# Seven moves in a one-core diffusion-trunk kernel: first attention scores, last head pair, first output products, last expert unit and its overflow test

## What is computed

```python
h = rmsnorm(x, g1) * (1 + sc1) + sh1          # sh, sc, gate rows from silu(cond) @ w_ada
z = h @ w_in                                   # columns of four mixers
y_f = fftn(u_f, axes=(1, 3), norm='ortho').real             # Fourier
y_l, y_s = rg_lru(...), gated_convolution(...)
q, k, v = latent_attention_inputs(...)         # 8 heads of 96; 640 keys for a latent token
o = softmax(q @ k.T * scale) @ v
br = stack([y_f @ w_pf, y_l @ w_pl, y_s @ w_ps, o @ w_pm])
out = sum(sigmoid(h @ w_gate) * br) @ w_out
x = x + gate1 * out
h = rmsnorm(x, g2) * (1 + sc2) + sh2
# top-1 of 4 groups, top-2 of its 8 experts; 32 experts of width 256
x = x + gate2 * sum_e combine_e * ((silu(h @ w1_e) * (h @ w3_e)) @ w2_e)
```

## Time and profile before

| | us |
|---|---|
| median of 3 runs | 1126.73 (1122.79 to 1127.68) |
| the profiled execution | 1123.43 |
| its span | 1121.5 |
| PE busy | 1007.0 (90%) |
| DVE busy | 388.4 (35%) |
| ACT, POOL busy | 225.3, 166.2 |
| mean granted TensorE clock | 0.959 |
| moved by DMA | 196.12 MB |

### The profile page before, as it was taken

How to read it: one execution, slowest core, us unless ns; L and a number is a source line. 1 busy time by engine, 2 the same in 40 slices (tenths; PEclk the granted TensorE clock), 3 DMA queues, 4 the chain that set the end, 5 groups by cost and what they waited for, 6 DMA issues and landing times.

```text
span 1121.5 us, 10795 instructions
## 1 busy us (share of the span) xinstructions
PE 1007.0 (90%) x4164; PEld 567.2 (51%) x4164; DVE 388.4 (35%) x845; ACT 225.3 (20%) x444; POOL 166.2 (15%) x160
## 2 busy tenths in 40 slices
PE   3899998999799989999999999989957897978875
PEld 1555544655455557777777777745533332322221
DVE  3314331135653523323233233317672232221222
ACT  3213630114254421101011011002111220211111
POOL 0000000010430013122132132100010111111111
PEclk9999999999889999999999999999978998998988
DMA  9634344100000152212213113092169999999993
GB/s 375 284 132 181 150 150 185 69 5 2 1 1 1 57 214 100 98 48 79 72 47 104 47 47 103 13 363 94 59 243 388 359 383 400 403 423 402 404 411 98
DMA packets 36163, 196.12 MB, mean 175 GB/s; under 512 B 7504, under 2 KB 11280, under 8 KB 25872
## 3 DMA queue, kind: packets, MB, share of 16 engines
q1 hardware_dynamic: 31200, 184.40, 41.9%
q0 software_dynamic: 4768, 10.50, 3.9%
q10 hardware_dynamic: 144, 0.52, 0.1%
HBM read 188.13 MB, written 14.09 MB: 180 GB/s over the span
## 4 chain that ended last, share of the span: by engine, by line
PE 82%; DMA 9%; issue 4%; DVE 3%; ACT 1%; POOL 0%; SPq 0%; POOLq 0%; DVEq 0%; ACTq 0%
PE psum L962 22%; PE psum L1143 9%; PE psum L697 8%; PE psum L979 8%; PE psum L1015 6%; PE psum L1159 4%; DMA r_bv<-in_w_e 4%; PE psum L813 3%; PE psum L899 3%; PE psum L698 2%; PE psum L706 2%; PE psum L913 2%; DMA r_w<-h_scratch,tab 2%; DMA r_w<-in_w_ada 2%; PE psum L923 2%
## 5 line engine op out<-in xcount | busy, mean ns | idle before, releaser
L962 PE MATMUL psum<-r_h,r_w 128*128 128x320 f32 x512 | 143.3, 433 | 1.7 <-DVE r_d L1824 1.7
L2248 POOL TENSOR_TENSOR r_w<-r_w 128x512 f32<-128x512 f32 x64 | 80.6, 1270 | 313.1 <-PE psum L962 237.2
L962 PEld LDWEIGHTS psum<-r_h,r_w 128*128 128x128 f32 x512 | 97.2, 190 | 42.3 <-DVE r_d L1824 2.0
L962 PE MATMUL psum<-r_ys,r_w 128*128 128x320 f32 x384 | 108.6, 432 | 0.0
L697 PE MATMUL psum<-r_h,r_w 128*128 128x512 f32 x192 | 98.9, 597 | 1.5 <-DVE r_h L1587 1.5
L962 PEld LDWEIGHTS psum<-r_ys,r_w 128*128 128x128 f32 x384 | 73.0, 190 | 30.4
L1414 ACT ACTIVATE r_bv<-r_bv 128x320 f32<-128x320 f32 x64 | 30.1, 470 | 273.2 <-DVE r_bv L1871 273.2
L1015 PE MATMUL psum<-r_w,r_bv 128*128 128x512 f32 x160 | 74.0, 609 | 3.4 <-DVE r_bv L1866 3.4
L698 PEld LDWEIGHTS psum<-r_h,r_w 128*128 128x128 f32 x192 | 36.5, 190 | 45.9 <-issue 45.9
L2259 POOL DMA_INDIRECT out_y<-r_bv,tab x17 | 26.8, 1576 | 211.7 <-DVE r_bv L2099 191.7
L979 PE MATMUL psum<-r_ys,r_w 128*128 128x320 f32 x192 | 55.6, 432 | 0.0
(11 more groups left out here) (378 smaller groups left out, 1624.4 us busy)
## 6 DMA issues: line engine op xcount, KB each, us to landing
r_a<-in_w_ada SPq DMA_DIRECT2D x8, 2048.0 KB, 7.9
r_w<-in_w_gate SPq DMA_DIRECT2D x32, 512.0 KB, 4.6
r_a<-in_w_e SPq DMA_DIRECT2D x6, 2048.0 KB, 32.3
r_c<-in_w_e SPq DMA_DIRECT2D x6, 2048.0 KB, 32.8
r_w<-in_w_e SPq DMA_DIRECT2D x5, 2048.0 KB, 35.9
r_ys<-in_w_e SPq DMA_DIRECT2D x4, 2048.0 KB, 35.4
r_bv<-in_w_e SPq DMA_DIRECT2D x4, 2048.0 KB, 37.5
r_h<-in_w_e SPq DMA_DIRECT2D x4, 2048.0 KB, 36.2
```

The lines of the kernel that those rows point to most:

```text
L962: ins = mm(gate_bank(u, n), w[:, k, :], x[:, k, :], start=(k == 0), stop=(k == HK - 1))
L2248: g.tensor_tensor(w_mix[n], x, y, op).then_inc(s_wm, 1)
```

## The change

1. `modulation(11)` moves from ahead of `fy0` to between `fy0` and `fy1`; `FRONT` changes accordingly.
2. PE's first two `scores` come ahead of the transposes `qt4`, each waiting only for its own slot's last drain; slot 2's drain is waited for at the first `probabilities_T`, `qt4`'s at the first unit that reads it. On DVE `take_queries(4)` comes behind the first two maxima. The three `prob` buffers get new homes, since `qt4`'s input is still in the old ones.
3. The last `inverse` comes behind the first `gate_product` of gate unit 0, and the waits for the mixers' outputs move to the first `branch`.
4. The first four k of the four first output pieces wait for 12 merges in place of 16, and each for its own bank (`s_gadd`); the wait for 16 stands behind them.
5. Unit 16's two `w13` are loaded as four halves, both lower halves first; the upper ones have a semaphore of their own, waited for ahead of the second half of `hidden`.
6. Unit 16 projects into slot 0 and no longer waits for `s_yd` 16; DVE copies its transposed hidden values ahead of scaling unit 15's result.
7. The overflow test comes one unit sooner, behind unit 14's `project`, on all engines; on PE it waits for `s_yd` 15. POOL's store of unit 15 moves behind the test, and the overflow body uses slot 1 in place of 3.

```diff
-                          "l11r", "l11i", "uf1", "ar10", "fa0", "fa1", "fa2", "fa3", "fa4", "ar11", "fy0", "fy1",
+                          "l11r", "l11i", "uf1", "ar10", "fa0", "fa1", "fa2", "fa3", "fa4", "fy0", "ar11", "fy1",
...
+Y_SLOT = [2] * LAST + [0]
...
-        prob = [r_t[:, 0:NT], r_t[:, NT:2 * NT], r_sq[:, 0:NT]]
+        prob = [r_t[:, H * QK:H * QK + NT], r_sq[:, 0:NT], r_d[:, 3 * NT:4 * NT]]
...
                 for i in AFTER[u]:
-                    load_w13(i)
+                    if i in AT[LAST]:
+                        load_piece(i, wexp[i % NBUF][0][:, 0:W13 // 2], 0, W13 // 2, w13_loaded[i % NBUF])
+                    else:
+                        load_w13(i)
+                for i in AFTER[u]:
+                    if i in AT[LAST]:
+                        load_piece(i, wexp[i % NBUF][0][:, W13 // 2:W13], W13 // 2, W13, w13_rest)
...
-            sp.wait_ge(s_Y, LAST)
+            sp.wait_ge(s_Y, LAST - 1)
             overflow(sp, n_x, load_chunk)
...
-            modulation(11)
             wait_drained(pe, *[f"fa{t}" for t in range(TT)])
...
             for j in range(2):
+                if j:
+                    modulation(11)
                 o = begin(f"fy{j}")
...
-            heads_T("qt4", KT + TT - 1)
-            for s in range(4):
-                pe.wait_ge(drained[s], LAST_IN_SLOT[s])
...
                 if i >= 2:
                     pe.wait_ge(s_prob, i - 1)
+                else:
+                    pe.wait_ge(drained[i], LAST_IN_SLOT[i])
+                if t == LT:
+                    wait_drained(pe, "qt4")
...
             for i in range(2):
                 scores(i)
+            heads_T("qt4", KT + TT - 1)
...
             values(H // 2 - 1)
-            inverse(H // 2 - 1, len(UNITS))
-            pe.wait_ge(s_oTd, 4)
-            pe.wait_ge(s_yl, 2)
-            pe.wait_ge(s_ys, 2)
...
                 gate_product(u, 0, w[:, 0, 0], low[:, :, lo_t])
+                if u == 0:
+                    inverse(H // 2 - 1, len(UNITS))
...
+            pe.wait_ge(s_mdone, GATE_UNITS - 4)
+            for i, added in enumerate((3, 5, 6, 7)):
+                pe.wait_ge(s_gadd, 7 * (GATE_UNITS - 1) + added)
+                output(i // 2, i % 2, range(0, 4))
             pe.wait_ge(s_mdone, GATE_UNITS)
-            for t in range(2):
-                for n in range(2):
-                    output(t, n, range(0, 4))
...
+                if u == LAST:
+                    pe.wait_ge(w13_rest, 16 * len(AT[LAST]))
                 hidden(H_SLOT[u % 2], halves, range(KD // 2, KD)).then_inc(s_A, 1)
...
-                if u:
+                if u and u < LAST:
                     pe.wait_ge(s_yd, u)
...
-                if u != LAST - 1:
+                if u != LAST - 2:
                     continue
-                pe.wait_ge(s_yd, LAST)
+                pe.wait_ge(s_yd, LAST - 1)
+                pe.wait_ge(s_xTd, LAST + 1)
                 pe.wait_ge(s_slot, 1)
                 n_x = pe.value_load(xinfo[0:1, XCH:XCH + 1], min_val=1, max_val=XCH)
...
-            take_queries(TT - 1)
...
             for i in range(2):
                 maxima(i)
+            take_queries(TT - 1)
...
+                if p == LAST - 1:
+                    take_gate_T(LAST)
                 for n in range(2):
                     ins = v.tensor_tensor(y_sb[:, p % 2, n * 512:(n + 1) * 512],
-                                          psum[:, 2, n * 512:(n + 1) * 512], slot_g2[n], ALU.mult)
+                                          psum[:, Y_SLOT[p], n * 512:(n + 1) * 512], slot_g2[n], ALU.mult)
...
-            put_rows(LAST - 1)
...
-                pool.wait_ge(y_stored[i], 16 * (LAST // 2))
+                pool.wait_ge(y_stored[i], 16 * (LAST // 2 - i))
...
             overflow(pool, n_x, chunk)
+            put_rows(LAST - 1)
             put_rows(LAST)
```

More of the change, by code:

```diff
@@ L598, in load_piece @@
                      else a["w_e"][e, :, lo:hi])
-                sp.dma_start(dst, w).then_inc(done[i % NBUF], 16)
+                sp.dma_start(dst, w).then_inc(done, 16)
             def load_w13(i):
@@ L906, in probabilities_T @@
                 n = TT if UNITS[i][1] < LT else 1
+                if i == 0:
+                    pe.wait_ge(drained[2], LAST_IN_SLOT[2])
                 pe.wait_ge(s_prob, i + 1)
@@ L976, in branch @@
                         pe.wait_ge(s_mrg, 4 * u)
+                    elif j == 0:
+                        pe.wait_ge(s_oTd, 4)
+                        pe.wait_ge(s_yl, 2)
+                        pe.wait_ge(s_ys, 2)
                     for n, part in enumerate((lo_t, hi_t)):
@@ L1151, in hidden_T, with project @@
                 return ins
-            def project(halves):
+            def project(halves, slot=2):
                 for n in range(2):
@@ L1197, in _ @@
                     pe.wait_ge(w2_loaded[i % NBUF], 16 * pieces_until(W2_PIECES, i))
-                if u:
+                if u and u < LAST:
                     pe.wait_ge(s_yd, u)
                 pe.wait_ge(s_hT, u + 1)
-                project([(lo, wexp[i % NBUF][1:], hT[:, u % 2, :, lo:lo + C]) for lo, i in zip((0, C), AT[u])]) \
+                project([(lo, wexp[i % NBUF][1:], hT[:, u % 2, :, lo:lo + C]) for lo, i in zip((0, C), AT[u])], Y_SLOT[u]) \
                     .then_inc(s_Y, 1)
-                if u != LAST - 1:
+                if u != LAST - 2:
                     continue
-                pe.wait_ge(s_yd, LAST)
+                pe.wait_ge(s_yd, LAST - 1)
+                pe.wait_ge(s_xTd, LAST + 1)
                 pe.wait_ge(s_slot, 1)
@@ L1214, in chunk @@
                     pe.wait_ge(x_w, x * 16)
-                    hidden(3, [(0, x_wexp, x_xgT)]).then_inc(x_A, 1)
+                    hidden(1, [(0, x_wexp, x_xgT)]).then_inc(x_A, 1)
                     pe.wait_ge(x_h, x)
-                    hidden_T(3, x_gate).then_inc(x_hf, 1)
+                    hidden_T(1, x_gate).then_inc(x_hf, 1)
                     pe.wait_ge(x_hT, x)
@@ L1511, in chunk @@
                     act.wait_ge(x_A, x)
-                    A(x_gate[0:C, :], psum[0:C, 3, 0:FE], ACT.Tanh, scale=0.5).then_inc(x_th, 1)
+                    A(x_gate[0:C, :], psum[0:C, 1, 0:FE], ACT.Tanh, scale=0.5).then_inc(x_th, 1)
                     act.wait_ge(x_yd, x)
@@ L2080, in hidden_dve, with take_gate_T @@
                 v.tensor_tensor(x, x, o[:, FE:2 * FE], ALU.mult).then_inc(s_hid, 1)
+            def take_gate_T(u):
+                dve.wait_ge(s_hf, u + 1)
+                v.tensor_copy(hT[:, u % 2, :, :], psum[:, H_SLOT[u % 2], 512:512 + 2 * P]
+                              .rearrange("p (f n) -> p f n", f=2)).then_inc(s_hT, 1)
             hidden_dve(0)
             for p in range(LAST + 1):
-                dve.wait_ge(s_hf, p + 1)
-                v.tensor_copy(hT[:, p % 2, :, :], psum[:, H_SLOT[p % 2], 512:512 + 2 * P]
-                              .rearrange("p (f n) -> p f n", f=2)).then_inc(s_hT, 1)
                 if p < LAST:
+                    take_gate_T(p)
                     hidden_dve(p + 1)
@@ L2110, in chunk @@
                     v.scalar_tensor_tensor(out=x_gate[0:C, :], in0=x_gate[0:C, :], scalar=1.0,
-                                           in1=psum[0:C, 3, 0:FE], op0=ALU.add, op1=ALU.mult).then_inc(x_g, 1)
+                                           in1=psum[0:C, 1, 0:FE], op0=ALU.add, op1=ALU.mult).then_inc(x_g, 1)
                     dve.wait_ge(x_g, x)
-                    v.tensor_tensor(x_gate[0:C, :], x_gate[0:C, :], psum[0:C, 3, FE:2 * FE], ALU.mult) \
+                    v.tensor_tensor(x_gate[0:C, :], x_gate[0:C, :], psum[0:C, 1, FE:2 * FE], ALU.mult) \
                         .then_inc(x_h, 1)
                     dve.wait_ge(x_hf, x)
-                    v.tensor_copy(x_hT_sb, psum[:, 3, 512:512 + 2 * P]
+                    v.tensor_copy(x_hT_sb, psum[:, 1, 512:512 + 2 * P]
                                   .rearrange("p (f n) -> p f n", f=2)[:, :, 0:C]).then_inc(x_hT, 1)
```

11 lines of the change are left out of this document (6 added, 5 removed).

## The result

The changed kernel takes **1108.24 us** (median of 4 runs, 1104.77 to 1111.29) beside 1126.74 for the kernel before: ratio 0.9849, 95% interval 0.9826 to 0.9871. The forecast was 1107.4. The profiled execution took 1108.71 with a span of 1106.8. One of all executions of the kernel before, beside the second group of experiments, took 3439 us; no ratio uses it.

The account below looks back on a forecast made before the run. PE and its waits bound the kernel up to the last output product, then a gapless weight stream and a tail. Gains of 4.3, 7.2, 1.7, 0.9 and 3.6 sum to 17.7, from 1125.1 to 1107.4 us; range 1100 to 1114.5.

Parts of the forecast that it names:

- The two regimes: Up to the last output product PE and its waits bound; from there a gapless weight stream, then a tail.
- the bound of 4.7: Upper bound for moving modulation 11 between the Fourier products, taking half of `ar11`'s 3.08 us; forecast 4.3.
- The third rival: Low clock at the attention's and output's starts: attention gives 4.2, output nothing; 3.9 us more, 1111.3; chance 0.15.
- 3 us to spare: In the tail, the last `w2` lands at 1101.6, with 3 us to spare.
- stalling jump: Rival: the moved overflow test's jump stalls PE ahead of `hidden(16)`, moving the tail by 6.3 us to 1113.7; chance 0.12.
- The sum: Gains of 4.3, 7.2, 1.7, 0.9 and 3.6 over the whole kernel add to 17.7 us.
- limit of 5.6 us: For the whole kernel's time, 0.5%, about what can be told from no change.
- fourth rival: The stream ends when it did, so only the tail's 3.6 us counts: 1121.5; chance 0.04.

Follow-up runs that it names:

- again: The changed kernel run once more without any edit; 1108.86 us, ratio 0.9852.
- m2r: The changed kernel with VectorE's wait for the two later broadcast rows moved behind its first residual addition; 1107.24 us.
- both: The changed kernel with the edits of `inside` and `m2r` together; 1105.64 us, ratio 0.9829.
- fill_both: `both` plus 18 small unused transposes on PE in the gaps ahead of the last values; 1102.61 us, ratio 0.9792.
- final: `fill_both` with the last inverse back ahead of the gates and more filling transposes in the front and at the attention's start; 1100.54 us, ratio 0.9781.
- inside: The changed kernel with PE's waits for s_yd and s_xTd moved from ahead of the overflow test into the overflow loop's body; 1108.81 us.
- early_load: `inside` with PE's load of the overflow flag moved sooner, behind unit 2's projection; 1108.69 us.
- scores_alone: The kernel before with only part 2 of the change; 1119.59 us, ratio 0.9959.
- fill_inverse_back: The changed kernel with filling transposes ahead of the last values and the last inverse back ahead of the gates; 1105.15 us.
- inverse_back: The changed kernel with the last inverse back ahead of the gates, the mixers' waits staying at the first branch; 1109.40 us.

## Why the prediction was right, step by step

**The two regimes** held. From the first streamed load to the last landing it was 278.6 before, 278.1 after, and 278.1 to 278.5 in `again`, `m2r`, `both`, `fill_both` and `final`. What was saved ahead of it moved it whole: 823.02 became 812.82. (`inside` and `early_load` had 281.0 and 279.4; `inside` shows one longer PE wait near the stream's start, 10.58 for a small transfer where `both` has 9.16; I did not follow it further.)

**Part 1**, forecast 4.3, gave 3.8. `ar11` took 1.93, as estimated; the profiles show 1.92 as its length at full clock, so the bound of 4.7, with half of 3.08, could not be reached. Of the missing 0.5, 0.3 is the gap behind `fa4` (1.09, where the step has 0.75), the rest the two `fy`, 7.48 and 7.41 instead of 7.3.

**Part 2**, forecast 7.2, gave 7.9 at its place, with scores at full clock as I chose. Its step left something out: the start of the attention was costed, its end was taken to follow unchanged. The last values lost 2.45 and the two short transposes ahead of them 0.3. `scores_alone` shows that loss to come with part 2: 4.6 net in time. What in part 2 brings it, the earlier start or the new buffers, stays open, and for the kernel before there is only one profile with the full clock there. The third rival (the clock falls where I keep it up) was right in kind and named the wrong places.

**Part 3**, forecast 1.7, gave 1.5 (the shift grew from 8.07 at the end of the last values to 9.52 at the end of the gates). The size was right and the cause wrong. The step gave the gain to the inverse's new place; the traces of `fill_inverse_back` and `inverse_back` have no gap ahead of the gates with the inverse back in its old place, so the waits' new place gives it, and the inverse's costs 0.3.

**Part 4**, forecast 0.9, gave 0.7: the shift grew from 9.52 at the end of the gates to 10.20 at the stream's start. The gap of 2.7, its cause and the slow products behind it (four took 3.58, the next four 1.88) came as worked out. `m2r` confirms the cause.

**Parts 5 to 7**, forecast 3.6, gave 4.1: `project(14)` ended 10.57 sooner, the end came 14.7 sooner. The order was as forecast: a gap of 2.86 (2.9 forecast), no gap ahead of `hidden_T(16)`, a projection of 3.65 instead of 5.37. Two steps were not right. The halves are worth 0.1 to 1.6 and not nothing. And the last `w2` did not have 3 us to spare in every execution: in `again` it was what ended last.

The **stalling jump** did not show. Scaling to `hidden(16)` took 1.28 with full DMA queues, 1.32 before with empty ones, and no time at all once the waits were gone. The Trainium skill's rule in "Runtime: NRT & Kernel Launch", Instruction fetch mechanics, speaks of a target outside what is fetched; no run here shows such a stall.

**The sum.** In the profiled pair: 3.8 + 7.9 + 1.5 + 0.7 + 4.1 + 0.4 (PE inside the stream, 10.20 to 10.57) = 18.4, less 2.8 of low clock and 0.8 of the front, is 14.8 beside 14.7 measured (1121.5 to 1106.8). The medians differ by 18.5: the profiled execution of before lay 3.3 below its median, and its front had no low clock. So the forecast of 17.7 was 3 too high for the pair that it was worked out on. That it lies within 1 us of the difference of the medians is luck: the other executions of the kernel before were slower by about what the end of the attention took, and no trace shows why. Parts 1, 4, 6 and 7 were read from the traces alone; no run isolates them. By the prediction's own limit of 5.6 us its fourth rival, a gain of 3.6, counts as no change, so its chances add up to 0.92 for faster and 0.06 for the same.

## What to carry to other kernels

A removed gap is worth its length only if the work behind it keeps its clock. After moving a stretch in time, read again the products behind every short gap in it, not only those at the seam. Where PE has only short waits, small products with unused results in those waits bought 2.45 us at one place; what they bought at two more is not shown. Before giving PE time in front of a saturated stream's last bytes, count the distance from the last landing to the end: here 12.8 us was the least, and what helped below that was an earlier start of the stream. When a step has two edits (a wait moved, work moved), price them apart.

## What the runs showed of the hardware

- The same 20 products behind the same gaps (0.84, 0.43, 0.37 us) ran at the higher clock level in the one profile of the kernel before and at the lower in all nine profiles of kernels that had part 2 and no filling ahead of them: 5.75 to 7.13 us instead of 4.51. With the gaps filled, 4.51 in four of four. At `xl0`, with nothing in the front edited, a gap of 1.53 gave the higher level in three profiles and the lower in ten (in one of these, `inside`, the gap was 1.70). The Trainium skill's page "TensorE: Matmul & The Clock Gate", section Part 1: The HAM clock gate, says that recent activity of the engine sets the level and that the point of change varies from run to run; the rows agree. Its section Loop structure matters more than you think leaves it to the loop nest whether matmuls stay at the higher level; here the same order gave both.
- A PE wait of 1.83 us ahead of the last projection left it at full clock in `both` (3.67) and not in `inside` (5.37).
- At the start of a trace the granted clock of the view is not the speed of PE: every first modulation product ran at about half speed (3.45 to 3.64 us instead of 1.92) at a granted 1.00.
- The load of the flag and the jump of the overflow test took no PE time in `inside`; the 1.3 us after DVE's scaling is there only when the test stands behind a wait.
